# Seven-product scheme from the fourth weight slot on in the feed-forward up projection, with Pool's first weight sum behind VectorE's last mix

## The chip, the cores and the metric

The kernel runs on one core of a Trainium2 chip. The core has five engines with instruction queues of their own: TensorE (PE in the rows; PEld is its weight load), VectorE (DVE), ScalarE (ACT), GpSimd (POOL) and SyncE (SP, which here only asks for weights). They meet at semaphores. The metric is the device time of the whole program in microseconds (us), median of the runs shown.

## The reference, cut to what matters

One inference step of a 4-layer decoder in float32, for a prompt of 256 rows and 8 x 8 sample rows, 320 rows together. Each layer has a token mixer and then this feed-forward, with D_MODEL = 1024 and D_FF = 2816:

```python
def conv_ffn(x, buf, p, l):
    u, buf_new = causal_conv(x @ p['ffn_w_up'][l], buf, p['ffn_conv_w'][l])
    u = u + p['ffn_conv_b'][l]
    return (jax.nn.silu(u[..., :D_FF]) * u[..., D_FF:]) @ p['ffn_w_down'][l], buf_new
...
f, fb = conv_ffn(rmsnorm(x, nw[2]), ffn_conv[l], p, l)
x = x + rmsnorm(f, nw[3])
```

The change touches only how a part of `x @ ffn_w_up` is computed.

## The kernel before

Activations lie transposed: a tile holds 128 features by 320 rows (256 of the prompt, 64 of the samples). X is the residual, H the normalised input, both 8 tiles.

**Weights.** The up projection reads its 1024 x 5632 weights in 22 slots of 256 columns (1 MB each); slot s is column pair c = s // 2 of half s % 2 (0: the gate, 1: the factor) and gives two output tiles, numbered n = 2s and 2s + 1 in `order`. SyncE asks for the slots in the order of `plan` into a ring of NS = 4 buffers of SBUF, and each request waits until the buffer's last user is done (`weight_used`).

**Slots 0 and 1** are multiplied by the input before its norm is known (`pe_first_tiles`), into four PSUM banks; VectorE then scales H (L398) and those four results (L950, L951, event `xp_first`).

**Ordinary slots** (2 and 3 before the change): 2 tiles x 8 blocks of K = 16 matmuls of 128 x 128 weights by 320 columns. ScalarE copies each tile from PSUM into XP, a ring of four tiles with room for the convolution's history (L880, L881).

**Seven-product slots** (`FASTS`: 4 to 21 before). The slot's 1024 x 256 weights and the 1024 x 320 input are each seen as 2 x 2 blocks, and Strassen's method in Winograd's form takes seven products of 4 matmuls x 160 columns, 28 in all, in the order m1, m6, m5, m7, m2, m3, m4 (`pe_fast_up`). It needs
- four sums of weight blocks, made by Pool (`half_sums`: L581 for m5, L583 for m6, L584 for m7, L586 for m3), into a ring of NSUM = 4;
- four mixes of input blocks, made once per layer by VectorE (`mixes`: L595, L596, L598, L600; events mix1, mix3, mix2, mix4), that m5, m7, m6 and m4 of the first such slot wait for;
- in three PSUM banks (fa, fb, fd): ScalarE's copy of m1 (S1C, L868), without which m2 may not add into fa; VectorE's U2 = m1 + m6 + m5 part (L1008) and TT (L1010), without which m3 doesn't start; C22 into XP (L994, L995), without which m4 doesn't start; then C11 by ScalarE (L887), C12 (L994, L995) and C21 (L1025) by VectorE.

**Around each slot** a hand-written order stands on ScalarE (`act_ffn`) and VectorE (`dve_ffn`). At step s ScalarE does the first taps of the convolution of slot s - 1 (L832, two tiles), then, if slot s has seven products, the copy S1C; at even s the sigmoids of a column pair (L851, L853, L855, twice); the tails (L841, L842); the copies of slot s or C11; and the sample states for slot s + 1 (L822, which wait for convolutions that free the XP tiles). At step s VectorE does the two convolution steps for both tiles of slot s - 1 (L984, L987), then U2 and TT of slot s, at even s the gate (L962, L970, L972), and C22, C12, C21. The first convolution stands behind the mixes in VectorE's queue.

**Pool** (`pool_ffn`) waits for the norm's factor, then runs through the slots of FASTS: four sums each, and now and then mixes for the down projection.

Of the kernel before, what the change touches and what calls it, by code (L numbers as in the profile page):

```python
# [182 lines left out]
class Signals:  # L183
# [18 lines left out]
    def at(self, name, step):  # L202
        return self.sem(SEMAPHORE_OF.get(name, name)), (self.values[name, step] if self.values else 1)


def build(nc, io, values, layers=DEPTH):
    ctx = ExitStack()
    with ctx:
        sig = Signals(nc, ctx, values)
        to, at = sig.to, sig.at  # L210
# [291 lines left out]
        def pe_out(pe, q, keys, k, ready, rhs, c0=0):  # L502

            for c, slot_keys in enumerate(keys, c0):
# [36 lines left out]
                for k0, rows in DOWN_ROWS]  # L541
# [3 lines left out]
        S1C, U2, TT, VV = [HALFSUM[:, i, :] for i in (0, 1)], HALFSUM[:, 2, :], HALFSUM[:, 3, :], HALFSUM[:, 4, :]  # L545

        UP = [(c, half) for c in range(11) for half in range(2)]
        FASTS = range(4, 22)
        summed = [key for l in range(layers) for key in
                  [("up", l, UP[s][1], UP[s][0]) for s in FASTS] + [("down", l, c, part) for c in range(4) for part in range(3)]]  # L550
        sum_of = {key: i for i, key in enumerate(summed)}
# [23 lines left out]
        def half_sums(eng, key, made):  # L575

            (a11, a12, a21, a22), (s1, s2, s3, s4) = quarters(key)
            eng.wait_ge(*at(f"slot{where[key] % NS}", key))
            if sums_before(key):
                eng.wait_ge(*at(*sums_before(key)))  # L580
            eng.tensor_tensor(s1, a21, a22, ALU.add).then_inc(*to(made["m5"], key))  # L581
            eng.wait_ge(*at(made["m5"], key))
            eng.tensor_tensor(s2, s1, a11, ALU.add).then_inc(*to(made["m6"], key))  # L583
            eng.tensor_tensor(s3, a11, a21, ALU.add).then_inc(*to(made["m7"], key))  # L584
            eng.wait_ge(*at(made["m6"], key))
            eng.tensor_tensor(s4, s2, a12, ALU.add).then_inc(*to(made["m3"], key))  # L586
# [3 lines left out]
        def mixes(eng, names, dst, b1, b2, key):  # L590

            mix1, mix2, mix3, mix4 = names
            b11, b12, b21, b22 = b1[:, :, 0:HN], b1[:, :, HN:NT], b2[:, :, 0:HN], b2[:, :, HN:NT]
            t1, t2, t3, t4 = dst
            eng.tensor_tensor(t1, b12, b11, ALU.subtract).then_inc(*to(mix1, key))  # L595
            eng.tensor_tensor(t3, b12, b22, ALU.subtract).then_inc(*to(mix3, key))  # L596
            eng.wait_ge(*at(mix1, key))
            eng.tensor_tensor(t2, b22, t1, ALU.subtract).then_inc(*to(mix2, key))  # L598
            eng.wait_ge(*at(mix2, key))
            eng.tensor_tensor(t4, b21, t2, ALU.subtract).then_inc(*to(mix4, key))  # L600
# [16 lines left out]
        def pe_fast_up(pe, l, c, half):  # L617
# [7 lines left out]
            for step in PRODUCTS:  # L625
# [6 lines left out]
                if step in POOL_SUM:  # L632
                    pe.wait_ge(*at(POOL_SUM[step], key))
                if step in UP_MIX and (c, half) == UP[FASTS[0]]:
                    pe.wait_ge(*at(UP_MIX[step], ("up", l)))
# [109 lines left out]
        def slot_key(l, s):  # L745
            return ("up", l, UP[s][1], UP[s][0])

        def xp_ready(l, n):

            c, half, j, m = order[n]  # L750
            if n < 4:
                return [("xp_first", (l, half, m))]
            if n // 2 not in FASTS:
                return [("xp", (l, half, m))]
# [3 lines left out]
        def pe_ffn(pe, l):  # L758
# [11 lines left out]
            for n, (c, half, j, m) in enumerate(order):  # L770
                if n < 4:
                    continue
                if n // 2 in FASTS:
                    if j == 0:
# [30 lines left out]
        def act_ffn(act, l):  # L805
# [18 lines left out]
            def first_taps(s):  # L824

                for n in (2 * s, 2 * s + 1):
                    c, half, j, m = order[n]
                    for step in xp_ready(l, n) + [("xp_state", (l, half, m))]:
                        act.wait_ge(*at(*step))
                    for step in tap_free(l, n):  # L830
                        act.wait_ge(*at(*step))
                    act.activation(tap_bank(l, n), XP[:, n % 4, 2:338], ACT.Identity,  # L832
                                   scale=par("ffn_conv_w", (l * 3 + 2) * 44 + half * FT + m),
                                   bias=par("ffn_conv_b", l * 44 + half * FT + m)).then_inc(*to("tap2", (l, half, m)))
# [25 lines left out]
            for s in range(len(UP) + 1):  # L860
                if s >= 1:
                    first_taps(s - 1)
                if s in FASTS:
                    key = slot_key(l, s)
                    act.wait_ge(*at("m1", key))
                    if s - 2 in FASTS:
                        act.wait_ge(*at("u2", slot_key(l, s - 2)))
# [52 lines left out]
        def pool_ffn(pool, l):  # L920
            pool.wait_ge(*at("rstd", 4 * l + 2))

            def down_mixes(c):

                part, a, b = MIXED[c]
                k0, kp = DOWN_ROWS[part][0], DOWN_ROWS[part][1] // 2
                pool.wait_ge(*at("hff", (l, 2 * c + 1)))
                mixes(pool, POOL_MIX, [DMIX[part][i][:, a:b] for i in range(4)], HFF[:, k0 + a:k0 + b, :],
                      HFF[:, k0 + kp + a:k0 + kp + b, :], ("down", l, part, c))

            for s in FASTS:
                half_sums(pool, slot_key(l, s), POOL_SUM)
                if s % 2 == 0 and s // 2 - 2 in MIXED:
                    down_mixes(s // 2 - 2)
            down_mixes(9)
            for c in range(4):
                for part in range(3):
                    half_sums(pool, ("down", l, c, part), POOL_SUM)
                    if (c, part) == (0, 1):
                        down_mixes(10)  # L940
# [2660 lines left out]
        @block_.gpsimd  # L3601
        def _(pool):
            for l in range(layers):
                if mixer_of(l) == "rwkv":
                    pool_rwkv_chunks(pool, l)
                elif mixer_of(l) == "mla":
                    pool_squares(pool, mq)
                    pool_mla(pool, l)
                else:
                    pool_squares(pool, gq)  # L3610
                    pool_gdn(pool, l)
                pool_squares(pool, 4 * l + 1)
                pool_squares(pool, 4 * l + 2)
                pool_ffn(pool, l)
                pool_squares(pool, 4 * l + 3)
# [44 lines left out]
```

## Time and profile before

| | us |
|---|---|
| median of 3 runs | 2848.35 (2845.24 to 2849.4) |
| the profiled execution | 2847.51 |
| its span, first to last instruction | 2845.8 |
| TensorE busy in it | 2712.3 (95%) |
| VectorE busy | 1429.7 (50%) |
| ScalarE busy | 1019.3 (36%) |
| Pool busy | 949.1 (33%) |

Line numbers in the rows are those of the kernel before. L363 is the helper that issues nearly every matmul, so its rows are told apart by their operands: `bank<-h,weights` with 128x320 is an ordinary matmul, `bank<-arena` with 128x160 a product on a weight sum and a mix. Each float32 matmul is two instructions of TensorE, which the trace counts singly. In the timeline, neighbours of the same line and operands are merged (also where their widths differ), and the bracket gives the idle time ahead of the first and what ended it. A timeline row's start is exact; the end of a matmul is modelled, so durations of TensorE are best read from start to start.

### The profile page before, as it was taken

The page shows a single profiled execution, that of the slowest core. Times are in us where ns is not written, and L with a number is a line of the kernel's source. Part 1 is how long each engine was busy: PE and PEld are TensorE (multiplying, and loading weights), DVE is VectorE, ACT ScalarE, POOL GpSimd, SP SyncE. Part 2 cuts the span into 40 slices and gives each one's busy share as a digit, 9 for nine tenths or more (in the row PEclk, how much of TensorE's full clock was granted, in tenths as well). Part 3 has the DMA queues.
Part 4 walks back from the last instruction along what each step waited for, and adds up shares of the span by engine and source line. Part 5 has one row for each costly group of instructions (what it writes and reads, how often), then busy time and mean ns, then how long its engine had stood idle before and what let it go on. Part 6 is the DMA issues. An engine that isn't in the chain of part 4 may idle for free.

```text
span 2845.8 us, 61457 instructions
## 1 busy us (share of the span) xinstructions
PE 2712.3 (95%) x23915; PEld 2264.9 (80%) x23915; DVE 1429.7 (50%) x3265; ACT 1019.3 (36%) x3029; POOL 949.1 (33%) x1025
## 2 busy tenths in 40 slices
PE   7999999999999999999999889899998999999998
PEld 4779769997766668998766777789995679867997
DVE  7665546622243316633542565536616875546641
ACT  2233235422432225422655344325512133324531
POOL 0000117773213206774100002647670000115773
PEclk9999999999999999999999999999999999999999
DMA  5420124444333223443433003534442330123442
GB/s 157 157 76 6 38 76 146 137 143 110 81 109 90 77 79 119 134 143 120 129 106 110 6 6 109 166 124 134 141 137 75 126 104 5 25 71 124 134 143 75
DMA packets 348475, 287.99 MB, mean 101 GB/s; under 512 B 74700, under 2 KB 344572, under 8 KB 347804
## 3 DMA queue, kind: packets, MB, share of 16 engines
q1 hardware_dynamic: 329264, 267.03, 30.5%
q10 hardware_dynamic: 14828, 14.93, 1.6%
q8 instruction: 192, 3.15, 0.5%
q0 software_dynamic: 4096, 2.11, 0.4%
q14 instruction: 95, 0.78, 0.1%
HBM read 263.29 MB, written 20.73 MB: 100 GB/s over the span
## 4 chain that ended last, share of the span: by engine, by line
PE 88%; DVE 5%; issue 3%; ACT 2%; POOL 1%; DMA 0%; ACTq 0%; POOLq 0%; DVEq 0%
PE bank L363 85%; PE bank L3237 1%; PE bank L3260 1%; DVE post_scaled L479 0%; DVE x L482 0%; PE bank L1667 0%; DVE arena L2904 0%; ACT squares L433 0%; DVE small L1482 0%; POOL arena L1711 0%; POOL rstd L422 0%; DVE h L461 0%; PE bank L1649 0%; DVE h L2046 0%; PE bank L2356 0%
## 5 line engine op out<-in xcount | busy, mean ns | idle before, releaser
L363 PE MATMUL bank<-arena 128*128 128x160 f32 (+7 forms) x6090 | 793.6, 293 | 13.3 <-DVE arena L2827 5.1
L363 PEld LDWEIGHTS bank<-arena 128*128 128x128 f32 (+2 forms) x6090 | 690.8, 175 | 38.2 <-issue 14.2
L363 PE MATMUL bank<-arena,weights 128*128 128x160 f32 (+4 forms) x3376 | 675.2, 358 | 8.8 <-DVE arena L1471 6.6
L363 PEld LDWEIGHTS bank<-arena,weights 128*128 128x128 f32 (+2 forms) x3376 | 533.3, 188 | 127.4 <-issue 22.6
L363 PE MATMUL bank<-h,weights 128*128 128x320 f32 (+2 forms) x2576 | 567.9, 373 | 8.4 <-ACT h L448 8.4
L363 PEld LDWEIGHTS bank<-h,weights 128*128 128x128 f32 (+1 forms) x2576 | 431.3, 189 | 127.0 <-issue 17.4
L1711 POOL TENSOR_TENSOR arena<-arena,consts 128x256 f32<-128x256 f32 x30 | 22.9, 762 | 824.8 <-DVE arena L2034 579.1
L363 PE MATMUL bank<-h,arena 64*64 64x64 f32 (+3 forms) x3288 | 217.2, 238 | 2.1 <-DVE h L2046 1.7
L581 POOL TENSOR_TENSOR arena<-weights 128x512 f32<-128x512 f32 x128 | 159.4, 1245 | 171.8 <-DMA weights<-ffn_w_up 82.9
L363 PEld LDWEIGHTS bank<-h,arena 64*64 64x64 f32 (+1 forms) x3288 | 191.0, 147 | 6.6 <-DVE h L2046 2.8
L583 POOL TENSOR_TENSOR arena<-arena,weights 128x512 f32<-128x512 f32 x128 | 160.4, 1253 | 10.0
L586 POOL TENSOR_TENSOR arena<-arena,weights 128x512 f32<-128x512 f32 x128 | 159.2, 1244 | 0.0
L832 ACT ACTIVATE bank<-arena,params 128x336 f32<-128x336 f32 x176 | 110.5, 634 | 119.9 <-issue 58.1
L706 DVE TENSOR_TENSOR small<-bank,small 128x160 f32<-128x160 f32 x20 | 6.5, 325 | 292.0 <-ACT small L688 292.0
L584 POOL TENSOR_TENSOR arena<-weights 128x512 f32<-128x512 f32 (+1 forms) x120 | 148.1, 1234 | 0.0
L3554 POOL DMA_DIRECT2D arena<-cache_mla_krope x128 | 68.6, 536 | 181.5 <-issue 181.3
L984 DVE SCALAR_TENSOR_TENSOR bank<-arena,params,bank 128x336 f32<-128x336 f32 x176 | 99.6, 566 | 15.4 <-ACT bank L832 15.2
L422 POOL TENSOR_TENSOR rstd<-rstd,squares 128x320 f32<-128x320 f32 x70 | 62.7, 896 | 120.2 <-ACT squares L433 115.2
L688 ACT ACTIVATE small<-bank 128x160 f32<-128x160 f32 x20 | 6.1, 304 | 265.6 <-PE bank L363 265.6
L479 DVE SCALAR_TENSOR_TENSOR post_scaled<-h,params,rstd 128x320 f32<-128x320 f32 x64 | 42.1, 658 | 113.9 <-ACT rstd L442 113.9
L363 PE MATMUL bank<-squares,arena 64*128 64x128 f32 (+2 forms) x736 | 86.0, 297 | 8.0 <-ACT arena L3402 6.9
L363 PE MATMUL bank<-squares,consts 128*128 128x320 f32 (+3 forms) x264 | 77.5, 416 | 12.9 <-ACT squares L433 11.0
(375 smaller groups left out, 3723.8 us busy)
## 6 DMA issues: line engine op xcount, KB each, us to landing
weights<-ffn_w_up SPq DMA_DIRECT2D x88, 1024.0 KB, 5.1
weights<-ffn_w_down SPq DMA_DIRECT2D x32, 1024.0 KB, 5.2
weights<-rw_wrkv SPq DMA_DIRECT2D x24, 1024.0 KB, 5.1
weights<-gdn_w_in SPq DMA_DIRECT2D x24, 1024.0 KB, 5.4
arena<-cache_mla_latent SPq DMA_DIRECT2D x108, 128.0 KB, 2.3
weights<-ffn_w_down SPq DMA_DIRECT2D x16, 768.0 KB, 4.4
weights<-rw_wo SPq DMA_DIRECT2D x8, 1024.0 KB, 5.1
weights<-gdn_wo SPq DMA_DIRECT2D x8, 1024.0 KB, 5.1
```

The source lines that it names most:

```text
L363: return pe.matmul(out, lhsT, rhs, start=first, stop=last, skip_group_check=True)
L422: pool.tensor_tensor(RS[:, 0, :], SQ[:, 0, :] if m == 1 else RS[:, 0, :], SQ[:, m % 4, :], ALU.add)\
L479: dve.scalar_tensor_tensor(out=PS[:, m % 2, :], in0=H[:, m, :], scalar=par("norm_w", q * 8 + m), in1=RS[:, 1, :], op0=ALU.mult, op1=ALU.mu ...
L581: eng.tensor_tensor(s1, a21, a22, ALU.add).then_inc(*to(made["m5"], key))
L583: eng.tensor_tensor(s2, s1, a11, ALU.add).then_inc(*to(made["m6"], key))
L584: eng.tensor_tensor(s3, a11, a21, ALU.add).then_inc(*to(made["m7"], key))
L586: eng.tensor_tensor(s4, s2, a12, ALU.add).then_inc(*to(made["m3"], key))
L832: act.activation(tap_bank(l, n), XP[:, n % 4, 2:338], ACT.Identity, scale=par("ffn_conv_w", (l * 3 + 2) * 44 + half * FT + m), bias=par("f ...
L984: dve.scalar_tensor_tensor(out=tap_bank(l, n), in0=XP[:, n % 4, 1:337], scalar=w(1), in1=tap_bank(l, n), op0=ALU.mult, op1=ALU.add).then_i ...
L3237: ins = pe.transpose(ps[:, j * P:j * P + P], page_rows(b, 4 * g + j)[:, ct * P:ct * P + P], ident)
L3260: ins = pe.transpose(ps[:, j * P:j * P + P], PSB[:, k * P:k * P + P], ident)
L3554: pool.dma_start(PGR[:, b % 2, j * ROPE:(j + 1) * ROPE], io["cache_mla_krope"][0][bass.ds(page, 1), :, :] .rearrange("a p c -> (a p) c")). ...
```

## The change

`FASTS` begins at 3 and no longer at 4: in each of the four layers slot 3 (column pair 1, factor half) is computed with seven products. Everything that asks whether a slot is in FASTS follows: Pool's sums and their ring (31 sets of sums per layer, where there were 30), TensorE's products and banks, ScalarE's and VectorE's steps, and the event that frees the slot's weight buffer. And in `pool_ffn` Pool waits for mix4 of the layer, the last of VectorE's four mixes, before its first weight sum.

```diff
@@ -545,7 +545,7 @@
         UP = [(c, half) for c in range(11) for half in range(2)]
-        FASTS = range(4, 22)
+        FASTS = range(3, 22)
         summed = [key for l in range(layers) for key in
                   [("up", l, UP[s][1], UP[s][0]) for s in FASTS] + [("down", l, c, part) for c in range(4) for part in range(3)]]
@@ -928,6 +928,7 @@
                 mixes(pool, POOL_MIX, [DMIX[part][i][:, a:b] for i in range(4)], HFF[:, k0 + a:k0 + b, :],
                       HFF[:, k0 + kp + a:k0 + kp + b, :], ("down", l, part, c))
 
+            pool.wait_ge(*at("mix4", ("up", l)))
             for s in FASTS:
                 half_sums(pool, slot_key(l, s), POOL_SUM)
```

Lines behind L930 move down by one. On ScalarE, from the states of slot 3 to the first taps of slot 3, the order before is (L832 the first taps of slot 2, L880 and L881 the copies of slot 3, L868 the copy S1C of slot 4):

```order
L822 ACTIVATE arena<-ffn_state 128x8x2 x2
L832 ACTIVATE bank<-arena,params 128x336 x2
L841 ACTIVATE arena<-arena 128x2
L842 ACTIVATE arena<-arena 128x16
L841 ACTIVATE arena<-arena 128x2
L842 ACTIVATE arena<-arena 128x16
L880 ACTIVATE arena<-bank 128x256
L881 ACTIVATE arena<-bank 128x8x8
L880 ACTIVATE arena<-bank 128x256
L881 ACTIVATE arena<-bank 128x8x8
L822 ACTIVATE arena<-ffn_state 128x8x2 x2
```

And in the changed kernel, at the same place (L868 is now the copy S1C of slot 3, L887 its C11):

```order
L822 ACTIVATE arena<-ffn_state 128x8x2 x2
L832 ACTIVATE bank<-arena,params 128x336 x2
L868 ACTIVATE small<-bank 128x160
L841 ACTIVATE arena<-arena 128x2
L842 ACTIVATE arena<-arena 128x16
L841 ACTIVATE arena<-arena 128x2
L842 ACTIVATE arena<-arena 128x16
L887 ACTIVATE arena<-bank 128x160
L822 ACTIVATE arena<-ffn_state 128x8x2 x2
```

The four copy instructions of slot 3 are gone, C11 stands in their place, and an S1C stands directly behind the first taps of slot 2.

On VectorE, from the second tile of slot 2 on, before (L984 and L987 the convolution steps of that tile, then of the two of slot 3, L1008 and L1010 U2 and TT of slot 4):

```order
L984 SCALAR_TENSOR_TENSOR bank<-arena,params,bank 128x336
L987 SCALAR_TENSOR_TENSOR arena<-arena,params,bank 128x336
L984 SCALAR_TENSOR_TENSOR bank<-arena,params,bank 128x336
L987 SCALAR_TENSOR_TENSOR bank<-arena,params,bank 128x336
L984 SCALAR_TENSOR_TENSOR bank<-arena,params,bank 128x336
L987 SCALAR_TENSOR_TENSOR bank<-arena,params,bank 128x336
L1008 TENSOR_TENSOR small<-bank,small 128x160
L1010 TENSOR_TENSOR small<-bank,small 128x160
```

And in the changed kernel, from the same tile on (each line number one higher):

```order
L985 SCALAR_TENSOR_TENSOR bank<-arena,params,bank 128x336
L988 SCALAR_TENSOR_TENSOR arena<-arena,params,bank 128x336
L1009 TENSOR_TENSOR small<-bank,small 128x160
L1011 TENSOR_TENSOR small<-bank,small 128x160
L995 TENSOR_TENSOR arena<-bank,small 128x96
L996 TENSOR_TENSOR arena<-bank,small 128x8x8
L995 TENSOR_TENSOR arena<-bank,small 128x96
L996 TENSOR_TENSOR arena<-bank,small 128x8x8
L1026 TENSOR_TENSOR arena<-bank,small 128x160
L985 SCALAR_TENSOR_TENSOR bank<-arena,params,bank 128x336
```

U2, TT, C22, C12 and C21 of slot 3 stand now between the convolutions of slot 2 and those of slot 3. Pool's queue has one more set of four sums in front, of slot 3, whose first waits for mix4.

## Rows read from the trace of the kernel before

**Rows 1.** The page: busy us, share, instructions; last, the chain's shares by engine

```profile
PE 2712.3 (95%) x23915; PEld 2264.9 (80%) x23915; DVE 1429.7 (50%) x3265; ACT 1019.3 (36%) x3029; POOL 949.1 (33%) x1025
...
PE 88%; DVE 5%; issue 3%; ACT 2%; POOL 1%; DMA 0%; ACTq 0%; POOLq 0%; DVEq 0%
```

**Rows 2.** Timeline of TensorE: start, us, engine, line, operation, xcount [idle before]

```profile
424.74 24.94 PE L363 MATMUL bank<-h,weights 128*128 128x320 f32 x96
449.52 3.42 PE L363 MATMUL bank<-arena 128*128 128x160 f32 x24
...
457.12 3.42 PE L363 MATMUL bank<-arena 128*128 128x160 f32 x24
```

**Rows 3.** Timeline of VectorE, the mixes of layer 0's activations

```profile
434.40 0.82 DVE L596 TENSOR_TENSOR arena<-h 128x640 f32<-128x640 f32 x1
435.14 0.82 DVE L598 TENSOR_TENSOR arena<-h,arena 128x640 f32<-128x640 f32 x1
436.00 1.77 DVE L600 TENSOR_TENSOR arena<-h,arena 128x640 f32<-128x640 f32 x1
437.69 0.56 DVE L984 SCALAR_TENSOR_TENSOR bank<-arena,params,bank 128x336 f32<-128x336 f32 x1
```

**Rows 4.** Timeline of Pool, its first weight sums of layer 0

```profile
435.62 1.46 POOL L581 TENSOR_TENSOR arena<-weights 128x512 f32<-128x512 f32 x1 [13.37 <-DMA weights<-ffn_w_up]
437.16 1.73 POOL L583 TENSOR_TENSOR arena<-arena,weights 128x512 f32<-128x512 f32 x1
...
453.84 1.27 POOL L581 TENSOR_TENSOR arena<-weights 128x512 f32<-128x512 f32 x1 [2.43 <-DMA weights<-ffn_w_up]
```

**Rows 5.** Timeline of ScalarE, a state copy and the taps of slot 2

```profile
439.97 0.23 ACT L822 ACTIVATE arena<-ffn_state 128x16 f32<-128x16 f32 x1 [0.85 <-DVE arena L987]
...
445.40 1.20 ACT L832 ACTIVATE bank<-arena,params 128x336 f32<-128x336 f32 x2
```

**Rows 6.** Timeline of ScalarE, the taps of slot 3 and slot 4's copy

```profile
449.34 1.19 ACT L832 ACTIVATE bank<-arena,params 128x336 f32<-128x336 f32 x2
450.46 0.29 ACT L868 ACTIVATE small<-bank 128x160 f32<-128x160 f32 x1
```

**Rows 7.** Timeline of VectorE, slots 3 and 4

```profile
450.01 0.57 DVE L984 SCALAR_TENSOR_TENSOR bank<-arena,params,bank 128x336 f32<-128x336 f32 x1 [1.66 <-ACT bank L832]
...
452.53 0.32 DVE L1010 TENSOR_TENSOR small<-bank,small 128x160 f32<-128x160 f32 x1
...
453.60 0.25 DVE L994 TENSOR_TENSOR arena<-bank,small 128x96 f32<-128x96 f32 x1
...
456.24 0.32 DVE L1025 TENSOR_TENSOR arena<-bank,small 128x160 f32<-128x160 f32 x1 [0.70 <-PE bank L363]
```

**Rows 8.** L600 on VectorE: count, ns min/median/max, first and last start

```profile
L600 DVE TENSOR_TENSOR arena<-h,arena x4: 1772/1773/1773, 436.0 to 2592.4; 128x640 f32<-128x640 f32 x4
```

**Rows 9.** Timeline of TensorE, the same place of layer 1

```profile
1077.89 24.94 PE L363 MATMUL bank<-h,weights 128*128 128x320 f32 x96
1102.67 3.42 PE L363 MATMUL bank<-arena 128*128 128x160 f32 x24
```

**Rows 10.** Stretches: us, busy (count) of each engine, TensorE's granted clock, DMA

```profile
1010.00:1012.00 2.00, 1.62 (x10) 1.28 (x11) 0.07 (x1) 2.00 (x8) 0.00 (x0) 0.81 0.00 0
1012.00:1014.00 2.00, 1.72 (x9) 1.29 (x8) 0.63 (x1) 1.48 (x6) 0.00 (x0) 0.50 0.00 0
1014.00:1016.00 2.00, 2.00 (x10) 1.76 (x9) 0.92 (x3) 0.27 (x1) 0.00 (x0) 0.84 0.03 8
```

**Rows 11.** Timelines of ScalarE and TensorE around two waits

```profile
412.12 0.56 ACT L448 ACTIVATE h<-x,params 128x320 f32<-128x320 f32 x1 [1.15 <-DVE x L482]
...
412.82 11.01 PE L363 MATMUL bank<-h,weights 128*128 128x320 f32 x40 [1.36 <-ACT h L448]
...
1010.34 2.43 PE L3260 MATMUL bank<-consts,arena 128*128 128x128 f32 x12 [2.07 <-ACT arena L3402]
```

**Rows 12.** Timeline of SyncE's queue: the request of slot 3's weights

```profile
408.54 0.37 SPq L3576 DMA_DIRECT2D weights<-ffn_w_up  x1
```

## The prediction, made before the result was known

> **What bounds the kernel now.** I read the page's busy shares first, then TensorE's order of time around the change, then the engines that feed it. TensorE is busy for 95% of the span, Pool for 33% [rows 1], and the chain of work that ended last is TensorE for 88% [rows 1]. In the feed-forward of a layer the timeline of TensorE is one unbroken run: 96 ordinary and first-product passes from 424.74, then group after group with no idle time in front [rows 2]. So in this stage a matmul pass that is saved is time that is saved, and a wait that is added is time that is added, as long as nothing else fills in. The four layers run it alike: the next layer has the same two marks, 96 passes from 1077.89 and the first mixed products 24.78 us later [rows 9]; in the first layer it is 449.52 - 424.74 = 24.78 too. I work one layer out and multiply by four.
>
> **What slot 3 costs TensorE.** Each fp32 matmul is two passes. From 424.74 the run holds 24 passes of the first tiles, 64 of slots 2 and 3 and 8 of slot 4's first product. Seven-product slots follow each other every 457.12 - 449.52 = 7.60 us [rows 2], so a product (8 of 56 passes) takes 1.087, and slot 4 began at 449.52 - 1.09 = 448.43. The 88 wide passes took 23.69 us, 0.269 each, an ordinary slot 32 x 0.269 = 8.61; slot 3 began at 439.82. As seven products it takes 7.61: **1.00 us less per layer**, 4.0 in all. That is the whole gain on offer.
>
> **What slot 3 now asks of the others, at that early place.** Its products go m1 at 439.82, m6 at 440.91, m5 at 441.99, m7 at 443.08, m2 at 444.17, m3 at 445.25, m4 at 446.34, if nothing waits. Three kinds of wait stand ahead of them.
>
> Pool's sums, for m6, m5, m7 and m3. The weights of slot 3 were asked for at 408.54 [rows 12], 28 us before Pool could start on them, where the seven-product slots behind take one such slot every 7.61 us; they are no limit. The new wait holds Pool until VectorE's last mix ends. That mix, L600, took 1.77 us in each layer [rows 8], and L598, of the same shape, 0.82 [rows 3]; Pool's first sum began at 435.62, between them, and Pool's own first two took 1.46 and 1.73 where a later one takes 1.27 [rows 4]. With Pool held I give L600 0.82 as well: it ends at 436.82, Pool starts at 436.9, and even with the slow spacing and length of today's second sum (1.54 after the first, 1.73 long) that one ends at 440.2. m6 wants it at 440.91: 0.7 us to spare at worst. Behind the held sum queue Pool's other sums; slot 4's follow four sums of 1.27 later, near 442, and are wanted from 451 on; nothing else of the stage waits on Pool, and no DMA is in its queue there. Pool gets 4 more sums per layer, 5.1 us on an engine that is idle for two thirds. The weight buffer of slot 3 is freed 1.8 us later than now, so Pool starts slot 7's sums, 453.84 today [rows 4], at about 455.7; TensorE wants them at 450.3 + 3 x 7.61 + 1.1 = 474.2. I cost all of this at nothing.
>
> ScalarE's copy S1C, for m2. ScalarE takes its work in order, and ahead of slot 3's copy (L868) stand the sigmoids of the first column pair, the copies of slot 2 and the first taps of slot 2 (L832), with L868 directly behind that L832. ScalarE worked without a gap from the state copy at 439.97 to the taps at 445.40 [rows 5], and that state copy waited for VectorE's second convolution. VectorE starts its convolutions when L600 is done: from L600's start to L984's was 1.69 [rows 3], while from L596's start to L598's, two mixes that Pool did not meet, it was 0.74. So all of it comes **0.95 us earlier**: taps at 444.45. In slot 4's case L868 began 1.12 after such a pair of taps and took 0.29 [rows 6], here 445.57 to 445.86. TensorE starts 0.14 after an ACT result (412.68 to 412.82, [rows 11]): m2 at 446.00, due 444.17. **Wait of 1.83 us.**
>
> VectorE's TT, for m3. In slot 4's case VectorE's L984 began 0.67 after ScalarE's taps (449.34 to 450.01), and from L984 to the end of L1010 it was 452.85 - 450.01 = 2.84 [rows 6, 7]. From 444.45 that gives 445.12 and 447.96, and 448.10 for TensorE; m3 is due 1.09 after m2, at 447.09. **Second wait, 1.01 us.** C22, for m4, comes some 0.4 later (L994 and its partner L995, the first 0.25 long [rows 7]) at 448.4, and m4 is due at 449.19: no wait.
>
> Slot 3 thus ends at 448.10 + 2.17 = 450.27, where before it ended at 448.43: **1.84 us later per layer**, 7.4 in four. For slot 4 I checked the same waits: ScalarE's copy of slot 4 follows the taps of slot 3, whose second waits for C21. L1025 began 0.20 after slot 4's end (457.12 - 1.09 = 456.03) and took 0.32 [rows 2, 7], so C21 of slot 3 is there at 450.8; the taps (half of 1.19) and the copy (0.29) [rows 6] with 0.2 for their starts make it 451.9, and it is wanted at 454.6. From there the pattern is that of every later slot, which runs without a gap. Nothing behind gives the 1.84 back, since there TensorE has no idle time to shrink [rows 2]. Banks: slot 3 takes three that VectorE read for the first tiles before its mixes; slot 4 takes two that ScalarE reads ahead of the taps of slot 2, so before 444.5; no wait.
>
> **The clock.** Two waits close together may cost more than themselves. One wait of 1.36 us, at 411.46, left the granted clock alone (the pace behind it is that of 40 passes in 11.01 us); a wait of 2.07 us before 1010.34 was followed by clock 0.81, 0.50 and 0.84 in three stretches of 2 us [rows 10, 11], full speed being 2.4 GHz and 0.50 the lower level, 1.2 GHz. Summed, 0.38 + 1.00 + 0.32 = 1.70 us lost if TensorE is busy all the while, and that is the upper price of one fall; the lower is 0.7, where the slow passes run into the second wait and use it up (1.70 - 1.01). My 1.83 and 1.01 with 1.09 of work between lie between the two rows, nearer to the second. I take a fall in two layers of four at 1.3 each, a little above the middle of the two prices: 2.6 us, with 0 and 6.8 as ends.
> The Trainium skill (TensorE: Matmul & The Clock Gate, section A second HAM failure mode: psum-queue depth-cycling) says that short idles between groups of matmuls can be enough to make the clock drop and return over and over. The row at 1010.34 agrees. By that rule every layer would fall, and the time would be the upper end of the waits' case below.
>
> **Sum.** 4 x 1.84 + 2.6 = 10.0 us on the profiled execution's 2847.5 (span 2845.8): 2857.5. The median of the runs shown is 0.8 above that execution, so 2858.4; I say **2858**.
>
> **Rivals.**
> (a) *The waits as worked out*, with the clock falling in none to all layers: +7.4 to +14.2, 2855.8 to 2862.6. Chance 0.76.
> (b) *Only the first wait counts*: TT turns out ready, because VectorE's two convolutions of slot 2 get through before m2 ends. Then 1.83 - 1.00 = 0.83 a layer, +3.3: 2851.7. For it: VectorE has the shorter list ahead. Against: the 2.84 us from L984 to the end of L1010 are four convolution steps back to back. Chance 0.10.
> (c) *The copies are in time*, the other side: no wait, -4.0, 2844.3, within 0.2% and not slower. It decides at S1C ending by 444.0 and TT by 445.1. For it: ScalarE was idle for 0.85 us before 439.97 [rows 5]. Against: that idle time ended with VectorE's L987, which comes no sooner than I have it, and 1.8 us more than the 0.95 would have to be found. Chance 0.08.
> (d) *Holding Pool does not quiet VectorE*: L600 stays at 1.77. Then nothing moves up by 0.95 and each layer loses 1.84 + 0.95 = 2.79, +11.2: 2859.6 without a fall of the clock. Against it: Pool's start is all that differs between L598 and L600. Chance 0.04.
> The Trainium skill (SBUF — State Buffer, section SBUF: two separate sides) calls the pair of ports that VectorE and Pool share an exclusive lock for a VectorE instruction with two SBUF inputs. By it (d) falls away; rows 3 and 4 agree.
> (e) A gain of over 0.2% needs 5.7 us, more than (c) at its best; 0.02 for what I don't see.
>
> **Numbers.** Forecast 2858, case (a). Range 2851 to 2863: it holds (a) with all its prices, (b) and (d), and leaves out (c) and (e), and what measurement adds at the top. A difference of 0.2% (5.7 us) is about what a measurement can tell from none. Slower: (a) and (d), less 0.03 for runs of (a) without a fall that measure below 5.7: 0.77. Same: (b), (c) and that 0.03: 0.21. Faster: 0.02.
>
> **What would show it.** In the profile after: L600 at 0.82, and L984 0.95 sooner; Pool's first L581 at 436.9; ordinary passes ending at 439.8; an idle time of TensorE ended by ScalarE's L868 near 446, and a second ended by VectorE's L1011 near 448, in each layer; slot 4 starting near 450.3 and no idle time behind it; in some layers a granted clock of 0.5 for three or four us from about 447. If m6 is the one that waits, for Pool's L583, my account of Pool is wrong; if there is no wait at m2, that of ScalarE is.

## The result, and the profile after

| us | before | changed |
|---|---|---|
| median | 2846.21 (2843.62 to 2849.4, 16 runs) | 2852.46 (2847.68 to 2855.75, 16 runs) |
| the profiled execution | 2847.51 | 2850.54 |
| its span | 2845.8 | 2848.9 |
| its mean granted clock | 0.987 | 0.989 |

The ratio of the times is 1.0019, with a 95% interval of 1.0013 to 1.0026; the means are 2846.43 and 2852.34, so the change costs **5.9 us, about 0.2%**. The forecast was 2858 and slower by more than 0.2%. The time lies in the range of 2851 to 2863, near its low end; the difference is about 0.2% and lies below the +7.4 us that was the least of the forecast case.

The page of the changed kernel answers to [rows 1]: TensorE is busy for less time and is a smaller part of the chain of work.

```profile
PE 2706.2 (95%) x24011; PEld 2269.8 (80%) x24011; DVE 1431.7 (50%) x3293; ACT 1019.1 (36%) x3021; POOL 966.8 (34%) x1041
...
PE 86%; DVE 6%; issue 3%; ACT 3%; POOL 1%; DMA 0%; ACTq 0%; DVEq 0%; POOLq 0%
```

TensorE at slot 3 of layer 1 (start, us, engine, line, operation, xcount, [idle before <- what ended it]), where before there was one unbroken run [rows 9]:

```profile
1096.75 3.42 PE L363 MATMUL bank<-arena 128*128 128x160 f32 x24
1101.78 1.35 PE L363 MATMUL bank<-h,weights 128*128 128x160 f32 x8 [1.61 <-ACT small L868]
1103.89 1.35 PE L363 MATMUL bank<-h,arena 128*128 128x160 f32 x8 [0.75 <-DVE small L1011]
1105.08 1.25 PE L363 MATMUL bank<-arena,weights 128*128 128x160 f32 x8
1106.17 1.25 PE L363 MATMUL bank<-h,weights 128*128 128x160 f32 x8
```

The 24 passes are m6, m5 and m7 (m1 stands ahead of them), then come m2, m3, m4, and the last row is m1 of slot 4. A product takes 1.087. So m2, due at 1096.75 + 3 x 1.087 = 1100.01, came 1.77 late; m3, due at 1101.78 + 1.09 = 1102.87, came 1.02 late. Slot 3 takes 1106.17 - 1095.66 = 10.51, before 8.61: **+1.90**. Layers 2 and 3 have the same two waits (1.61 and 0.75, 1.60 and 0.75 in the brackets). Layer 0 has them and something more:

```profile
441.84 3.42 PE L363 MATMUL bank<-arena 128*128 128x160 f32 x24
446.87 1.35 PE L363 MATMUL bank<-h,weights 128*128 128x160 f32 x8 [1.61 <-ACT small L868]
448.98 2.20 PE L363 MATMUL bank<-h,arena 128*128 128x160 f32 x8 [0.76 <-DVE small L1011]
450.98 2.12 PE L363 MATMUL bank<-arena,weights 128*128 128x160 f32 x8
452.93 1.25 PE L363 MATMUL bank<-h,weights 128*128 128x160 f32 x8
```

Here m3 and m4 take 2.0 us each, nearly double. The view by stretches (columns as in [rows 10]; the granted clock is the third number from the right) says why:

```profile
446.00:448.00 2.00, 1.13 (x8) 1.11 (x8) 1.85 (x4) 1.23 (x7) 2.00 (x3) 1.00 0.03 9
448.00:450.00 2.00, 1.25 (x7) 1.02 (x6) 1.28 (x5) 0.54 (x3) 1.92 (x2) 0.83 0.00 0
450.00:452.00 2.00, 2.00 (x9) 2.00 (x8) 0.39 (x2) 0.31 (x1) 2.00 (x3) 0.50 0.00 0
452.00:454.00 2.00, 2.00 (x13) 2.00 (x13) 0.83 (x3) 0.78 (x2) 2.00 (x2) 0.81 0.00 0
```

The clock was at its lower level, 1.2 GHz, from about 449.3 to 452.7. Slot 3 takes 452.93 - 440.75 = 12.18 here, 1.67 more than in the other layers.

The other engines, in order of time. VectorE's mixes and first convolution, against [rows 3]:

```profile
435.35 0.82 DVE L596 TENSOR_TENSOR arena<-h 128x640 f32<-128x640 f32 x1
436.09 0.82 DVE L598 TENSOR_TENSOR arena<-h,arena 128x640 f32<-128x640 f32 x1
436.94 0.83 DVE L600 TENSOR_TENSOR arena<-h,arena 128x640 f32<-128x640 f32 x1
437.68 0.57 DVE L985 SCALAR_TENSOR_TENSOR bank<-arena,params,bank 128x336 f32<-128x336 f32 x1
```

L600 fell from 1.77 to 0.83. This execution ran 0.94 later than that of before ahead of the layer (425.68 against 424.74), and the first convolution starts at the same 437.7: it comes 0.95 sooner. Pool starts right behind the mix, at full pace, against [rows 4]:

```profile
437.89 1.27 POOL L581 TENSOR_TENSOR arena<-weights 128x512 f32<-128x512 f32 x1 [14.70 <-issue]
439.24 1.27 POOL L583 TENSOR_TENSOR arena<-arena,weights 128x512 f32<-128x512 f32 x1
```

And ScalarE reaches the copy S1C behind the taps of slot 2, against [rows 5]:

```profile
445.40 1.21 ACT L832 ACTIVATE bank<-arena,params 128x336 f32<-128x336 f32 x2
446.51 0.31 ACT L868 ACTIVATE small<-bank 128x160 f32<-128x160 f32 x1
```

**Where the time is in these two profiles.** Slot 3 adds 1.90 x 3 + 3.57 = 9.3 us, while the span grows by 3.1. I lined the two timelines of TensorE up, row by row, and took the offset (changed minus before, us) along the way: +0.94 ahead of layer 0's slots (from the first 25 us of the program, where start-up varied by some 2 us between profiles), +4.50 behind slot 3, +2.70 by 1022, +4.59 behind slot 3 of layer 1, +6.56 behind that of layer 2, +4.89 by 2297, +0.93 by 2488, +2.82 behind that of layer 3, +3.03 at the end. Slot 3 adds what was counted in each layer, and between the slots of one layer and the next, in stages that the change doesn't touch, 0.94 + 9.3 - 3.0 = 7.2 us are given back on balance. The largest such step is in the token mixer of the last layer. TensorE's timeline there in the kernel before:

```profile
2473.28 1.00 PE L363 MATMUL bank<-arena 128*128 128x64 f32 x8
...
2477.84 1.08 PE L363 MATMUL bank<-arena 64*64 64x512 f32 x4 [1.91 <-DVE arena L2118]
...
2485.91 1.19 PE L363 MATMUL bank<-arena 64*64 64x64 f32 x8
```

The same three operations in the changed kernel:

```profile
2478.59 1.00 PE L363 MATMUL bank<-arena 128*128 128x64 f32 x8
...
2481.84 1.07 PE L363 MATMUL bank<-arena 64*64 64x512 f32 x4 [0.60 <-DVE arena L2119]
...
2486.84 1.19 PE L363 MATMUL bank<-arena 64*64 64x64 f32 x8
```

The same work starts 5.31, then 4.00, then 0.93 later than before. The first step, 1.31, is a shorter wait for VectorE, and VectorE's own row there names a store of the state that it must let land before it writes again. Before:

```profile
2476.16 0.69 DVE L1676 TENSOR_TENSOR arena<-bank,small 128x512 f32<-128x512 f32 x1 [3.66 <-DMA out_p_rwkv_wkv<-squares]
```

In the changed kernel:

```profile
2480.16 0.69 DVE L1677 TENSOR_TENSOR arena<-bank,small 128x512 f32<-128x512 f32 x1 [2.34 <-DMA out_p_rwkv_wkv<-squares]
```

The second step, 3.07, is the clock, which was low for 6.8 us behind the longer wait and not at all behind the shorter. Stretches of before:

```profile
2478.00:2482.00 4.00, 4.00 (x26) 3.31 (x24) 1.51 (x3) 0.27 (x2) 1.04 (x1) 0.62 0.00 0
2482.00:2486.00 4.00, 4.00 (x20) 1.76 (x21) 1.12 (x2) 0.82 (x2) 0.00 (x0) 0.53 0.05 12
```

And the stretch of the changed kernel behind its wait:

```profile
2482.00:2486.00 4.00, 4.00 (x36) 2.81 (x36) 2.54 (x5) 0.38 (x3) 1.04 (x1) 1.00 0.02 4
```

That is 4.4 of the 7.2 us. Before also had falls near 806, 1011 and 2260 that the changed profile hasn't; they go with the steps from 4.50 to 2.70 and from 6.56 to 4.89. The one at 1011 is instructive: the wait of 2.07 us that I priced a fall by [rows 10, 11] is there again, of the same length, at 1013.81, and this time the clock stayed up:

```profile
1013.81 1.97 PE L3261 MATMUL bank<-consts,arena 128*128 128x128 f32 x12 [2.07 <-ACT arena L3403]
```

The stretches there, with the granted clock at 1.00 throughout:

```profile
1012.00:1016.00 4.00, 1.88 (x12) 1.25 (x12) 1.47 (x4) 3.11 (x11) 0.00 (x0) 1.00 0.00 0
1016.00:1020.00 4.00, 3.49 (x19) 3.15 (x20) 0.92 (x3) 1.22 (x3) 0.00 (x0) 1.00 0.02 4
```

So a wait of a given length is followed by a fall of the clock in one execution and not in another. The questions for the experiments: are the steps of the mechanism (Pool held, S1C, TT) the causes, and is what was given back elsewhere chance, or a share of every delay?

### The profile page after: what moved, and what is told of

Same layout as the page of the kernel before. It is cut to its first block, busy times and chain, and to the rows that moved or that the text cites. A ratio compares the mean times of both kernels' runs of the same rounds, so it can differ in the third digit from the quotient of the medians.

```text
span 2848.9 us, 61724 instructions
## 1 busy us (share of the span) xinstructions
PE 2706.2 (95%) x24011; PEld 2269.8 (80%) x24011; DVE 1431.7 (50%) x3293; ACT 1019.1 (36%) x3021; POOL 966.8 (34%) x1041
## 4 chain that ended last, share of the span: by engine, by line
PE 86%; DVE 6%; issue 3%; ACT 3%; POOL 1%; DMA 0%; ACTq 0%; DVEq 0%; POOLq 0%
PE bank L363 83%; PE bank L3238 1%; PE bank L3261 1%; DVE post_scaled L479 0%; DVE x L482 0%; DVE arena L2905 0%; PE bank L1668 0%; POOL arena L1712 0%; ACT bank L832 0%; ACT squares L433 0%; DVE small L1483 0%; POOL rstd L422 0%; DVE h L461 0%; DVE h L2047 0%; PE bank L1650 0%
## 5 line engine op out<-in xcount | busy, mean ns | idle before, releaser
L363 PE MATMUL bank<-arena 128*128 128x160 f32 (+7 forms) x6186 | 805.8, 293 | 12.0 <-DVE arena L2828 5.1
L363 PEld LDWEIGHTS bank<-arena 128*128 128x128 f32 (+2 forms) x6186 | 703.3, 175 | 36.6 <-issue 14.1
L363 PE MATMUL bank<-h,weights 128*128 128x320 f32 (+2 forms) x2512 | 543.8, 368 | 14.8 <-ACT h L448 8.4
L363 PEld LDWEIGHTS bank<-h,weights 128*128 128x128 f32 (+1 forms) x2512 | 416.0, 189 | 124.2 <-issue 17.4
L363 PE MATMUL bank<-h,arena 64*64 64x64 f32 (+3 forms) x3320 | 223.7, 239 | 5.1 <-DVE small L1011 3.0
L581 POOL TENSOR_TENSOR arena<-weights 128x512 f32<-128x512 f32 (+1 forms) x132 | 164.0, 1242 | 163.6 <-DMA weights<-ffn_w_down 48.3
L363 PEld LDWEIGHTS bank<-h,arena 64*64 64x64 f32 (+1 forms) x3320 | 196.3, 148 | 10.7 <-DVE small L1011 4.0
L583 POOL TENSOR_TENSOR arena<-arena,weights 128x512 f32<-128x512 f32 (+1 forms) x132 | 163.7, 1240 | 10.4
L586 POOL TENSOR_TENSOR arena<-arena,weights 128x512 f32<-128x512 f32 (+1 forms) x132 | 164.4, 1246 | 0.0
L832 ACT ACTIVATE bank<-arena,params 128x336 f32<-128x336 f32 x176 | 110.8, 634 | 130.9 <-issue 70.5
L584 POOL TENSOR_TENSOR arena<-weights 128x512 f32<-128x512 f32 (+1 forms) x124 | 153.3, 1236 | 0.0
L363 PE MATMUL bank<-squares,consts 128*128 128x320 f32 (+3 forms) x264 | 78.1, 420 | 12.5 <-ACT squares L433 10.7
```

Source lines behind the costliest of these rows:

```text
L363: return pe.matmul(out, lhsT, rhs, start=first, stop=last, skip_group_check=True)
```

## The experiments

Three series, each on one chip beside runs of the kernel before: its means there were 2847.22 (22 runs), 2846.37 (29) and 2846.86 (18). Line numbers in the diffs are left out.

### The two parts apart

**Pool's wait alone**, against the changed kernel:

```diff
-        FASTS = range(3, 22)
+        FASTS = range(4, 22)
```

**Seven products from slot 3 without the wait**:

```diff
-            pool.wait_ge(*at("mix4", ("up", l)))
             for s in FASTS:
```

> The kernel before plus Pool's wait for mix4 alone; seven products still from slot 4 on. Theory W (the time comes from slot 3's two waits for ScalarE's S1C and VectorE's TT): TensorE gets no new wait, so no change, within 1 us of before; L600 falls from 1.77 to 0.83 us and VectorE's and ScalarE's chain behind it comes 0.95 us sooner without use. Rival P (holding Pool costs time, since its sums come late): slower by over 2 us, with TensorE idle ahead of a product on a weight sum.

> The changed kernel without Pool's wait for mix4. Theory W: Pool does slot 3's sums as soon as the norm is known and slot 4's during L600, which takes 1.77 us again; ScalarE's and VectorE's chain is 0.95 later, both waits end 0.95 later, and it is 4 x 0.95 = 3.8 us slower than the changed kernel, +9.7 on before. Rival P: faster than the changed kernel.

The wait alone: 2846.2 (11 runs), ratio 0.9999 (0.999 to 1.0008). L600 takes 0.82 and the first convolution starts at 437.65, but nobody waited for it: free, and worth nothing by itself. Without the wait: 2874.92 (4 runs), ratio 1.0097 (1.0082 to 1.0113), **28 us slower**, where I had expected about 10. VectorE in that kernel:

```profile
435.31 1.89 DVE L596 TENSOR_TENSOR arena<-h 128x640 f32<-128x640 f32 x1
437.12 1.88 DVE L598 TENSOR_TENSOR arena<-h,arena 128x640 f32<-128x640 f32 x1
439.04 1.78 DVE L600 TENSOR_TENSOR arena<-h,arena 128x640 f32<-128x640 f32 x1
```

Pool beside it, at the same times:

```profile
434.80 1.70 POOL L581 TENSOR_TENSOR arena<-weights 128x512 f32<-128x512 f32 x1 [3.57 <-DMA weights<-ffn_w_up]
436.58 1.74 POOL L583 TENSOR_TENSOR arena<-arena,weights 128x512 f32<-128x512 f32 x1
438.28 1.85 POOL L584 TENSOR_TENSOR arena<-weights 128x512 f32<-128x512 f32 x1
```

And TensorE, whose m2 is the second row:

```profile
440.09 3.42 PE L363 MATMUL bank<-arena 128*128 128x160 f32 x24
449.92 2.50 PE L363 MATMUL bank<-h,weights 128*128 128x160 f32 x8 [6.41 <-ACT small L868]
```

My expectation took over from [rows 3] that one mix is slowed. With slot 3's sums made early, Pool's sums for slot 4 run beside three mixes, each of 1.8 to 1.9 in place of 0.82. And Pool's four sums for slot 3, from 425.24 on, run beside VectorE's scaling of H, one row up to 432.78, which comes ahead of the mixes:

```profile
425.19 7.59 DVE L398 TENSOR_TENSOR h<-h,rstd 128x320 f32<-128x320 f32 x8 [3.41 <-ACT rstd L442]
```

In the first profile of the changed kernel that scaling began at 426.95 and ended at 432.84, 5.89 after its start and not 7.59: that is 1.7 us, and the three mixes are 3.1. Together they are the 4.8 by which the wait for S1C grows, from 1.61 to 6.41. The clock is low for 6.8 us in slot 3 of every layer, where the changed kernel has 3.4 in some. The second half of the change is what makes the first bearable.

### The change once more

> The changed kernel again, as the measure for the others of this call. +5.9 us on before (mean of the runs so far), and in the trace two waits of about 1.6 and 0.75 us idle in slot 3 of each layer. If the clock falls behind them by chance, the number of layers with granted clock 0.5 in slot 3 differs from that of the first trace (one).

2852.29 (11 runs; one of them took 6416.91, was disturbed and is in no mean here), ratio 1.0015 (1.0006 to 1.0024), mean +4.8. Its profile has span 2854.5 at clock 0.985, with falls in slot 3 of layers 0 and 2, and outside the feed-forward near 809, 1014 and 2270, where the first profile of the changed kernel had none. So falls outside slot 3 differ between two executions of the same kernel, too.

### The waits taken away

S1C is issued ahead of the tails in step 2 (its bank is complete by then), and U2, TT and C22 ahead of the convolutions of slot 2, for slot 3 only:

```diff
 # act_ffn, step 2, ahead of the tails
+                if s == 2:
+                    act.wait_ge(*at("m1", slot_key(l, 3)))
+                    act.activation(S1C[1], of(("fa", slot_key(l, 3)))[:, 0:HN], ACT.Copy).then_inc(*to("s1c", slot_key(l, 3)))
 # dve_ffn, step 3, ahead of the convolutions; left out behind them
+                if s == 3:
+                    u2_tt(s, key)
```

Both:

> The changed kernel with, for slot 3 alone, ScalarE's S1C moved ahead of the tails of step 2 and VectorE's U2, TT and C22 ahead of the convolutions of slot 2. Theory W: both waits of TensorE go, slot 3 takes 7.6 us and not 10.5, 4 x 1.0 us faster than before: -4 us. If the loss lies elsewhere, it stays at about +6.

> The changed kernel with the copy S1C ahead of slot 1's part of the tails and U2, TT and C22 ahead of the convolutions of slot 2, for slot 3, once more: 2836.6 in its first series, 10 less than the kernel before, where the passes saved are worth 4.0 less. If the other 6 were falls of the clock avoided by position, they may be there again, since the position is the same: 2835 to 2840. If they were chance of the chip: 2841 to 2844.

2836.63 (6 runs), ratio 0.9963 (0.9951 to 0.9976); again 2837.98 (7 runs), 0.9965 (0.9954 to 0.9976). This **beats both kernels**, by 0.36% and some 0.55%. TensorE is unbroken again (here of the first of them, layer 0):

```profile
440.11 3.42 PE L363 MATMUL bank<-arena 128*128 128x160 f32 x24
443.37 1.25 PE L363 MATMUL bank<-h,weights 128*128 128x160 f32 x8
444.45 1.25 PE L363 MATMUL bank<-h,arena 128*128 128x160 f32 x8
```

By count this is worth 4.0 us, which is what I had expected, and 10 were measured. Lined up with the profile of before, the feed-forward gives 1.01 us in each layer, as counted; the rest comes outside it, the largest part between the feed-forwards of layers 2 and 3, where the late store stands that the profile of before has.

Only the copy S1C, then only U2, TT and C22:

> The changed kernel with only ScalarE's S1C of slot 3 moved ahead of the tails of step 2. By the prediction's second term m3 still waits for TT at the old moment, behind the convolutions of slot 2: m2 starts in time, the whole idle time moves in front of m3 (about 2.8 us), and the time stays that of the changed kernel, +5.9 us on before. Rival (only the first wait counts): 1.8 us a layer faster than the changed kernel, below before.

> The changed kernel with only VectorE's U2, TT and C22 of slot 3 moved ahead of the convolutions of slot 2; S1C stays behind the taps. m2 waits as before (1.6 us idle), m3 no more: 1.0 us a layer faster than the changed kernel, about +2 us on before. Rival (the second wait costs nothing): as the changed kernel.

The copy alone gives 2854.96 (7 runs), ratio 1.0035 (1.0022 to 1.0048), mean +8.3: no better than the change, as expected, and rather worse. The wait moves in one piece in front of m3:

```profile
442.89 1.25 PE L363 MATMUL bank<-h,weights 128*128 128x160 f32 x8
446.96 2.50 PE L363 MATMUL bank<-h,arena 128*128 128x160 f32 x8 [2.82 <-DVE small L1015]
```

VectorE's steps alone give 2847.04 (12 runs), ratio 1.0005 (0.9996 to 1.0014), mean +1.2, expected about +2. The first wait stays and the second is gone:

```profile
445.45 1.35 PE L363 MATMUL bank<-h,weights 128*128 128x160 f32 x8 [1.61 <-ACT small L868]
446.64 1.25 PE L363 MATMUL bank<-h,arena 128*128 128x160 f32 x8
```

So the two waits have two causes, of which TT is the later one: mending only S1C gains nothing, mending only TT takes the second wait.

### The waits filled

The changed kernel with six extra products of 160 columns ahead of m2 and three ahead of m3, which nobody reads:

```diff
+                if (c, half) == UP[FASTS[0]] and step in ("m2", "m3"):
+                    pe.wait_ge(*at("rstd_ln", 4 * l + 2))
+                    for _ in range(6 if step == "m2" else 3):
+                        mm(pe, of(("norm", 4 * l + 2))[:, 0:HN], ones, C[:, 0:HN], True, True)
```

> The changed kernel with 6 matmuls of 128x160 on constants in TensorE's first wait and 3 in its second, into an unused PSUM bank; they add work that nobody reads and fit in the idle time. Theory W + clock (the granted clock falls behind the waits in some layers, 1.7 us each): no fall in slot 3 any more, 2 to 4 us faster than the changed kernel. If the fall is not caused by the idle time, or costs nothing on average, the time is that of the changed kernel within 1 us.

2849.69 (12 runs), ratio 1.0017 (1.0005 to 1.0029), mean +3.9, which is 1.7 below that of the changed kernel on the same chip (2850.3 and 2852.0), with a standard error of 1.5; I had expected 2 to 4. Slot 3 still takes 10.50 us, and the clock falls in slot 3 of none of the four layers, against three of eight in the two profiles of the changed kernel. That is what the idle time as the cause of these falls would give, but four layers of one profile don't prove it:

```profile
442.81 1.79 PE L363 MATMUL bank<-consts 128*128 128x160 f32 x12
444.58 1.35 PE L363 MATMUL bank<-h,weights 128*128 128x160 f32 x8
445.77 0.98 PE L363 MATMUL bank<-consts 128*128 128x160 f32 x6
446.69 1.35 PE L363 MATMUL bank<-h,arena 128*128 128x160 f32 x8
```

### What a delay of known size is worth

The kernel before with extra products, which nobody reads, between slots 2 and 3: seven in each layer (1.9 us, 7.6 in all), fourteen in each (15.2), and 28 in layer 0 alone (7.6):

```diff
+                if n == 6:
+                    pe.wait_ge(*at("rstd_ln", q))
+                    for _ in range(7):
+                        mm(pe, of(("norm", q))[:, 0:HN], ones, C[:, 0:HN], True, True)
```

> The kernel before with 7 matmuls of 128x160 on constants (1.9 us of TensorE, no idle time) between slots 2 and 3 of each layer; they add work that nobody reads. If a delay in the feed-forward adds up, as the prediction says: 4 x 1.9 = +7.6 us. If later stages give part of any delay back (as the changed kernel's +5.9 against its 9.3 of added time in slot 3 suggests), +4 to +6.

> The kernel before with fourteen extra products of 160 columns between slots 2 and 3 of every layer (work that nobody reads): 4 x 3.8 = 15.2 us of added TensorE time with no idle time. With seven of them (7.6 us) the median rose by 2 to 3. Theory A, added time counts fully on average and the small figure came from falls of the granted clock in other stages that came or went by chance of position: the median rises by 12 to 18. Theory B, the program hides a fixed share (some slack in another stage absorbs it): 4 to 8.

> The kernel before with 28 extra products (7.6 us, nobody reads them) between slots 2 and 3 of layer 0 alone: the same added work as seven in each layer, at one place. Theory A (only the position of the later stages against the clock's falls differs): between 4 and 11, and other falls of the clock than in the kernel with seven per layer. Theory B (each layer absorbs about 1.3 us behind slot 3): 7.6 less one such share, about 6.

Measured: 2848.87 (12 runs), ratio 1.0006 (0.9997 to 1.0015); 2862.54 (5 runs), 1.0043 (1.0027 to 1.006); 2852.5 (11 runs), 1.0019 (1.001 to 1.0028). In means: +2.5, +13.1 and +5.0 (standard errors 1.1, 2.2 and 1.1), for 7.6, 15.2 and 7.6 us of work that TensorE surely did. The first is below both of its expectations. A share that grows with the delay is refuted, since the double dose costs five times the single one. A fixed share of 1.3 us hidden in each layer, 5.1 in all, isn't refuted by these times: it would give 10.1 and, once, 6.3. The profiles refute it. Lined up with that of before, the padding shifts TensorE by 1.90 in each of the four layers, by 3.80 in each, and by 7.61 once, and nothing of that is lost up to the next slots. From the feed-forward of layer 0 to that of layer 1, and so on to the end, the offset of the kernel with seven extra then changes by +2.1, +0.6, -1.5 and +0.4, that of the one padded once by -0.9, +0.2, -3.4 and 0.0: steps of both signs, the larger ones at falls of the clock and at the store near 2478, and no constant share.

> The same kernel without waits in slot 3, with the seven extra products (1.9 us a layer, 7.6 in all, nobody reads them) ahead of slot 3: theory A: 7.6 above it, plus or minus some 4 for falls of the clock elsewhere, so 2840 to 2848. Theory B (a fixed share hidden): 2839.

This last one was built wrongly. Slot 3 has seven products in it and leaves the loop ahead of the edit, so no extra product was issued (its profile has none), and it is a third series of the kernel with both waits taken away: 2837.62 (6 runs), ratio 0.9969 (0.9956 to 0.9981). It says nothing on the dose, but shows how well a mean repeats: 2836.57, 2836.69 and 2837.36.

**Time split by the clock.** Each run comes with the mean granted clock of its span. Its time multiplied by that is the time that it would take at full clock, roughly (idle time is scaled too), and the rest is what the low clock took. The clock is given to 0.001, 2.8 us, so only means are of use: the differences below have standard errors of 0.6 to 1.3 us at full clock and of 1.1 to 1.8 for the low clock. Differences of means against before on the same chip:

| kernel | slot 3 and padding, by count | time | at full clock | low clock |
|---|---|---|---|---|
| the change, again | +7.6 | +4.8 | +6.0 | -1.2 |
| Pool's wait alone | 0 | -0.7 | -0.4 | -0.3 |
| without Pool's wait | | +27.4 | +13.8 | +13.6 |
| S1C early | +8.3 | +8.3 | +4.4 | +3.9 |
| U2, TT, C22 early | +3.5 | +1.2 | +2.1 | -0.9 |
| both early, three series | -4.0 | -10.7, -10.2, -9.5 | -5.4, -6.2, -7.3 | -5.3, -3.9, -2.2 |
| waits filled | +7.6 | +3.9 | +8.4 | -4.4 |
| before, 7 extra a layer | +7.6 | +2.5 | +6.9 | -4.4 |
| before, 14 extra a layer | +15.2 | +13.1 | +10.8 | +2.3 |
| before, 28 extra once | +7.6 | +5.0 | +5.9 | -0.9 |

(The first column is worked out from the profiles: four times what slot 3 and the padding take beyond 8.61, in layers without a fall of the clock.) The seven extra products did add their 7.6, within the error; 4.4 us less of low clock elsewhere stand against them. The time follows the count far better at full clock than as measured, though mostly some 1 to 3 us below it, and for S1C early and the double padding 4. One place explains a part of that: the late store at 2477.84 and the wait of 1.8 to 1.9 us behind it stand in three of the fourteen profiles, those of before, Pool's wait alone and the filled waits; in the eleven others the wait there is 0.60 or 0.61. That is 1.3 us of waiting and up to 3.1 us of low clock that the profile of before has and most others don't. With one profile of most kernels, these runs don't show whether the late store belongs to the kernel or to the execution.

## Why the prediction was right and wrong, point by point

- **The gain of 1.00 us a layer**: right. Slot 3 without waits ran at the seven-product pace, as the kernel with both waits taken away shows in every layer.
- **Pool held, all of it 0.95 sooner**: right. L600 took 0.83, the first convolution came 0.95 sooner, and the second sum was there before m6. The rival that Pool doesn't quiet VectorE is out. The Trainium skill (SBUF — State Buffer, section SBUF: two separate sides) calls the shared pair of ports an exclusive lock for a VectorE instruction with two SBUF inputs, against a Pool instruction that reads SBUF; the traces agree, with 0.82 without Pool and 1.77 to 1.89 beside it.
- **First wait, S1C**: 1.83 predicted, 1.77 measured. **Second, TT**: 1.01 and 1.02. **No wait for m4, none in slot 4**: right. Net +1.84 predicted, +1.90 measured. The rivals of one wait or none are out, by the profile and by taking each wait away.
- **The clock in slot 3**: I had falls in two layers of four at 1.3 each, 2.6 in all. The two profiles have one and two falls, at 1.67 where it was measured: near the upper price (1.70), since m3 and m4, busy throughout, ran at the low level. Filling the waits is a measure of them: 1.7 us, with a standard error of 1.5. Three falls in eight layers at 1.67 are 2.5 for four layers, so within slot 3 the size was about right. The Trainium skill (TensorE: Matmul & The Clock Gate, section A second HAM failure mode: psum-queue depth-cycling) describes a kernel in which frequent short idles between groups of matmuls made the clock swing between its two levels. The rule that the prediction drew from it, a fall in every layer, is not borne out: three falls in eight layers.
- **"Nothing behind gives the 1.84 back"**: this is the step that failed. It holds within the feed-forward, where the offset stays to the end of the stage. It does not hold for the program: I priced falls of the clock only where the change adds waits, and took the low clock of all other stages as fixed, though my own rows showed one there [rows 10]. Those falls come and go, between kernels and between executions of one kernel. In its second series, beside runs of before on the same chip, the change costs 4.8 where my sum had 10.0. Of these 5.2 the clock is 3.8 (1.2 us less for it than before, where I had 2.6 more) and the part at full clock 1.4 (6.0 for 7.4). With standard errors of 1.5 and 0.8, the 2.6 on balance is out, while -1.2 can't be told from nothing, nor 6.0 surely from 7.4.
- **The base**: 2848.35 was the median of three runs; that of 16 is 2846.21. That alone puts the forecast 2.1 too high; with the sum it makes the 5.5 by which 2858 missed 2852.46.
- **The chances**: the case (a) was right by its waits (0.76), with no cost of the clock on balance. By the number alone it was luck that the time fell in the range: 2852.46 lies below all of (a) and next to the 2851.7 of rival (b), one wait only, for which the range reached down to 2851. What rules (b) out is the profile, which has both waits in each layer. I took 0.03 from "slower by over 0.2%" for that; with falls elsewhere counted in as plus or minus 4 us, a measured difference of 0.2% or less needed a much larger share, some 0.4.

**What stays open**: what decides whether a wait of about 2 us brings the clock down (the same wait near 1010 did in one profile and not in the other); why the store near 2477 lands late in some executions; and why, at full clock, 14 extra products cost only 10.8 for 15.2 and S1C early only 4.4 for 8.3. The share of the 10 us gained with both waits gone that is luck of position against the kernel before can't be told from these runs: about 4 is saved work, and the three series agree with one another, so in this program as it stands it is a gain.

## What to carry to other kernels

When a scheme with more steps is started earlier, list for each product which copy or mix releases it and what stands ahead of that on its engine: here a copy of ScalarE's and VectorE's U2, TT and C22, put ahead of the tails and convolutions, turned +0.2% into -0.36%, while moving the copy alone gained nothing. Where two engines slow each other, one wait that orders them can be free by itself and save 22 us once their work would meet. In a program whose clock falls in a dozen places, give every sum an error of some 4 us from places that the edit doesn't touch, and look at time and mean granted clock together before believing a small difference.

## What the runs showed of the hardware that I had not expected

- The same wait of 2.07 us was followed by 3.4 us at the lower clock level in one execution and by none in another.
- Padding TensorE with 7.6 us of work nobody reads cost 2.5 us, while the low clock took 4.4 us less in the whole program than before; the same 7.6 us in one place cost 5.0 (standard errors 1.1 for the two costs and 1.4 for the clock).
- VectorE's sum of two 128x640 tiles takes 0.82 us alone and 1.77 to 1.89 beside Pool's 128x512 sums, which take 1.70 to 1.85 then in place of 1.27: both engines lose. VectorE's scaling of H, eight sums of 128x320, took 7.59 us beside Pool's sums and 5.89 without, waits included.
- A state store that landed 1.3 us later made TensorE wait 1.91 in place of 0.60, and the fall of the clock behind it cost 3.07 more.
